# A two-layer-pair transformer kernel: the block before the last ends ahead of the last at six norms, and the last block goes by halves of the tokens

## The reference, cut to what matters

```python
def rms_norm(x, g):
    xf = x.astype(jnp.float32)
    y = xf * lax.rsqrt(jnp.mean(xf * xf, axis=-1, keepdims=True) + RMS_EPS) * g.astype(jnp.float32)
    return y.astype(x.dtype)
...
        h = h + mix_out
        h = h + conv_glu_ffn(rms_norm(h, norm_ffn_g[layer]), ffn_up[layer], ffn_conv_w[layer],
                             ffn_conv_b[layer], ffn_down[layer])
...
        h = h + g1 * y_lat
        h = h + g2 * conv_ffn(modulate(rms_norm_2(h, norm_ffn[i]), sh2, sc2), ffn_w_up[i], ffn_conv[i], ffn_w_down[i])
```

## Time and profile before

| | |
|---|---|
| median of 3 runs | 3118.66 us (3114.68 to 3126.62) |
| profiled execution, its own time | 3126.0 us |
| its span in the trace | 3124.2 us |
| mean granted TensorE clock | 0.978 of full speed |
| TensorE matmuls busy | 3029.7 us, 97% of the span |
| VectorE, ScalarE, GpSimd busy | 58%, 42%, 17% |
| memory traffic | 284.32 MB, mean 91 GB/s |

### The profile page before, as it was taken

The page is one execution under the profiler, slowest core; times in us unless marked ns, Lnnn a source line. Parts: engine busy times, 40 slices in busy tenths (PEclk is TensorE's granted clock), DMA queues, the critical chain, the costliest instruction groups (busy, mean ns, idle before and its releaser), DMA issues.

```text
span 3124.2 us, 46510 instructions
## 1 busy us (share of the span) xinstructions
PE 3029.7 (97%) x19324; PEld 2667.5 (85%) x19324; DVE 1822.9 (58%) x2664; ACT 1309.7 (42%) x2229; POOL 519.5 (17%) x464
## 2 busy tenths in 40 slices
PE   6999999999999999999999999998999999999999
PEld 6987878799999989998999987666888878878887
DVE  7675545448858563563876865664544543365353
ACT  4464555524323254673322355553332332343232
POOL 0002222123203200001311322101211201112020
PEclk9899989899999999999999999999999999999999
DMA  3210000014545422003554542101222222223222
GB/s 107 77 50 35 1 1 1 36 48 169 185 154 188 131 103 88 8 1 130 183 183 163 180 153 68 41 1 54 95 95 88 93 91 94 97 79 98 86 93 94
DMA packets 79554, 284.32 MB, mean 91 GB/s; under 512 B 8528, under 2 KB 9296, under 8 KB 78576
## 3 DMA queue, kind: packets, MB, share of 16 engines
q1 hardware_dynamic: 79344, 281.35, 27.1%
HBM read 274.96 MB, written 6.36 MB: 90 GB/s over the span
## 4 chain that ended last, share of the span: by engine, by line
PE 92%; DVE 4%; ACT 2%; issue 1%; DMA 0%; POOL 0%; SPq 0%; DVEq 0%; ACTq 0%; POOLq 0%
PE psum L345 64%; PE psum L2611 2%; PE psum L1193 2%; PE psum L839 2%; PE psum L1783 2%; PE psum L1214 2%; PE psum L1984 2%; PE psum L1225 1%; PE psum L1222 1%; PE psum L1966 1%; PE psum L1957 1%; PE psum L782 1%; DVE xt L682 1%; PE psum L2605 1%; PE psum L503 1%
## 5 line engine op out<-in xcount | busy, mean ns | idle before, releaser
L302 DVE TENSOR_TENSOR wlo<-wraw,whi 128x1024 fp32r<-128x1024 f32 (+2 forms) x398 | 508.6, 1299 | 629.7 <-ACT whi L295 620.6
L295 ACT CAST whi<-wraw 128x1024 fp32r<-128x1024 f32 (+2 forms) x398 | 396.2, 1022 | 515.4 <-PE psum L345 483.5
L426 DVE CUSTOM_DVE_ANT_0 araw<-araw,cond 128x1024 f32<-128x1024 f32 x112 | 181.2, 1655 | 0.0
L345 PE MATMUL psum<-f0xh,whi 128*128 128x264 f32 x704 | 143.8, 286 | 5.5 <-DVE f0xl L540 3.9
L345 PE MATMUL psum<-f1xh,whi 128*128 128x258 f32 x704 | 142.4, 284 | 5.6 <-DVE f1xl L540 3.8
L345 PE MATMUL psum<-f2xh,whi 128*128 128x512 f32 x352 | 140.1, 398 | 4.2 <-DVE f2xl L536 4.2
L345 PE MATMUL psum<-f3xh,whi 128*128 128x512 f32 x352 | 139.9, 397 | 4.2 <-DVE f3xl L536 4.2
L345 PE MATMUL psum<-f0xh,wlo 128*128 128x264 f32 x704 | 143.4, 285 | 0.0
L345 PE MATMUL psum<-f0xl,whi 128*128 128x264 f32 x704 | 143.0, 285 | 0.0
L345 PE MATMUL psum<-f1xh,wlo 128*128 128x258 f32 x704 | 142.3, 284 | 0.0
L345 PE MATMUL psum<-f1xl,whi 128*128 128x258 f32 x704 | 141.9, 283 | 0.0
(11 more groups left out here) (509 smaller groups left out, 8605.7 us busy)
## 6 DMA issues: line engine op xcount, KB each, us to landing
wraw<-d_w SPq DMA_DIRECT2D x357, 512.0 KB, 3.3
araw<-d_ada SPq DMA_DIRECT2D x112, 512.0 KB, 3.3
wraw<-d_w SPq DMA_DIRECT2D x32, 384.0 KB, 3.4
hn<-d_h SPq DMA_DIRECT2D x4, 528.0 KB, 7.6
hres<-d_h SPq DMA_DIRECT2D x1, 2112.0 KB, 8.5
spill<-hres SPq DMA_DIRECT2D x1, 2112.0 KB, 7.4
hres<-spill SPq DMA_DIRECT2D x1, 2112.0 KB, 9.1
cond<-d_cond SPq DMA_DIRECT2D x2, 1024.0 KB, 4.8
```

Source lines behind the costliest of these rows:

```text
L295: e.copy(whi[0:rows, n % NH, 0:kt * cols], wraw[0:rows, n % NR, 0:kt * cols]).then_inc(*w_hi.up(n))
L302: e.tensor_tensor(wlo[0:rows, n % NH, 0:kt * cols], wraw[0:rows, n % NR, 0:kt * cols], whi[0:rows, n % NH, 0:kt * cols].bitcast(F32), ALU. ...
L345: ins = e.matmul(psum[0:bw, b0 + nb * len(sl) + si, 0:ln], l_ if z == 2 else h_, (xp.lo if z == 1 else xp.hi)[:, k, o:o + ln], start=k == ...
L426: e.tensor_tensor_reduce(out=w, in0=w, in1=self.c[:, col, :], scale=1.0, scalar=0.0, op0=ALU.mult, op1=ALU.add, accum_out=ada[:, ly, blk, ...
```

## The change

Six parts, at the six norms that follow a projection (r0 is left as it is, but for its written form):

- In the last chunk of the last pair, TensorE goes through all k for block 6 first, then all k for block 7, and raises a semaphore of its own (`lin6`) when block 6 is complete.
- VectorE adds block 6 when `lin6` is up, and block 7 in two halves of the tokens, with a semaphore for the first half (`res7`).
- ScalarE squares block 7 in two halves.
- TensorE's sums go by halves of the tokens: the two halves of a sum have PSUM banks of their own at 512 tokens too, and the last sum waits for each half of the square alone and tells its first half (`n_ss7`).
- ScalarE's first logarithm waits for the first half of the sums, the second for the second.
- VectorE calls `ready` before it waits for the factor, and multiplies block 0 in two halves, each after its half of the factor.

```diff
@@ lin_pe
                     e.wait_ge(*w_lo.at(n))
-                    for i in range(cnt):
+                    apart = block6 is not None and j == pairs - 1 and k0 + cnt == kt
+                    for i, nb in sorted(((i, nb) for i in range(cnt) for nb in range(bpp)), key=lambda x: x[::-1] if apart else x):
                         k = k0 + i
-                        if j == 0:
+                        if j == 0 and nb == 0:
                             need(e, k)
...
+                        if apart and nb == 0 and i == cnt - 1:
+                            ins.then_inc(*lin6.up(block6))
                     ins.then_inc(*w_used.up(n))
@@ the squares and the root
+        LAST = {"f0": "wo", "sb": "f0b", "f1": "sbo", "f2": "wino", "sc": "f2b", "f3": "scout"}
...
+        def rms_square_last(e, t, src, sq, ntok):
+
+            e.wait_ge(*rms_added(t, 2))
+            half = ntok // 2
+            e.wait_ge(*res7.at(LAST[t]))
+            e.activation(sq[:, 2, 0:half], src(7)[:, 0:half], ACT.Square).then_inc(*n_sq7.up(t))
+            e.wait_ge(*res.at(LAST[t], 7))
+            e.activation(sq[:, 2, half:ntok], src(7)[:, half:ntok], ACT.Square).then_inc(*n_sq.up(t, 7))
+
         def rms_root(e, t, ntok, rt, bank):
-            e.wait_ge(*n_ss.at(t, 2))
             for h in range(2):
+                e.wait_ge(*(n_ss7.at(t) if t in LAST and not h else n_ss.at(t, 2)))
@@ the sums
         def rms_psum(ntok, bank, h):
+            return psum[:, bank + h, 0:ntok // 2]
+
+        def rms_pe(e, t, ntok, sq, bank):
             half = ntok // 2
-            return psum[:, bank + h, 0:half] if ntok > 512 else psum[:, bank, h * half:(h + 1) * half]
...
+                for h in range(2):
+                    if t in LAST and i == 2:
+                        e.wait_ge(*(n_sq.at(t, 7) if h else n_sq7.at(t)))
+                    elif not h:
+                        e.wait_ge(*(n_sq.at(t, 5 + i) if i else rms_added(t, 5)))
+                    ins = e.matmul(rms_psum(ntok, bank, h), ones, sq[:, i, h * half:(h + 1) * half], start=i == 0, stop=i == 2)
+                    if h:
+                        ins.then_inc(*n_ss.up(t, i))
+                    elif t in LAST and i == 2:
+                        ins.then_inc(*n_ss7.up(t))
@@ norm_dve
+            half = ntok // 2
+            ready(e)
+            e.wait_ge(*n_rf.at("rc", t, 0))
+            e.scalar_tensor_tensor(out=tmp[:, 0, 0:half], in0=src(0)[:, 0:half], scalar=gain(0), in1=rt[:, 0:half], op0=ALU.mult,
+                                   op1=ALU.mult).then_inc(*n_t0.up(t))
             e.wait_ge(*n_rf.at("rc", t, 1))
-            ready(e)
-            norm_t(e, t, src, rt, gain, tmp, 0)
+            e.scalar_tensor_tensor(out=tmp[:, 0, half:ntok], in0=src(0)[:, half:ntok], scalar=gain(0), in1=rt[:, half:ntok],
+                                   op0=ALU.mult, op1=ALU.mult).then_inc(*n_t.up(t, 0))
@@ add_dve and ffn_dve: the additions, now in one function
+        def add_block(e, t, tag, h_, ntok, gate, j, p, place):
+            nb = 2 * j + p
+            if nb == 6 and t in LAST.values():
+                e.wait_ge(*lin6.at(t))
+            else:
+                e.wait_ge(*w_used.at(last_chunk(tag, j)))
...
+            if nb == 7 and t in LAST.values():
+                half = ntok // 2
+                for i in range(2):
+                    hh = h_[:, 7, i * half:(i + 1) * half]
+                    pp = ps[:, i, :] if ntok > 512 else ps[:, 0, i * half:(i + 1) * half]
+                    up = res.up(t, 7) if i else res7.up(t)
```

More of the change, by code:

```diff
@@ L323, in __init__, with lin_pe @@
                 self.lo = put(name + "l", [rows, kt, ntok], F32R)
-        def lin_pe(e, tag, x, pairs, ntok, need, room, kt=8, bpp=2, set0=0, parts=None, sets=8, mid=None, after=None):
+        def lin_pe(e, tag, x, pairs, ntok, need, room, kt=8, bpp=2, set0=0, parts=None, sets=8, mid=None, after=None,
+                   block6=None):
             sl = parts or [(x, o, ln) for o, ln in splits(ntok)]
@@ L444, in program @@
         n_rf = sig("n_rf", [(s, t, h) for t in RMS for s in ("rt", "rc") for h in range(2)])
+        LAST = {"f0": "wo", "sb": "f0b", "f1": "sbo", "f2": "wino", "sc": "f2b", "f3": "scout"}
+        lin6 = sig("lin6", [(s,) for s in LAST.values()])
+        res7 = sig("res7", [(s,) for s in LAST.values()])
+        n_sq7 = sig("n_sq7", [(t,) for t in LAST])
+        n_ss7 = sig("n_ss7", [(t,) for t in LAST])
+        n_t0 = sig("n_t0", [(t,) for t in LAST])
         def rms_added(t, k):
@@ L483, in act, with rest @@
                     rms_square(e, self.t, self.src, self.sq, self.there, (0, 1) if j == 2 else range(2, 6))
-            def rest(self, e):
+            def rest(self, e, ntok):
                 e.preload_act_table_set("natural_log_exp_and_others")
-                rms_square(e, self.t, self.src, self.sq, self.there, (6, 7))
+                rms_square(e, self.t, self.src, self.sq, self.there, (6,))
+                rms_square_last(e, self.t, self.src, self.sq, ntok)
         def splits_and_squares(e, tag, sqs):
@@ L1587, in ffn_pe @@
                        lambda e, j: room(e, j, 15 * half + 11), kt=11, set0=15 * half + 11,
-                       mid=F.tail.pe if F.tail and half else None)
+                       mid=F.tail.pe if F.tail and half else None,
+                       block6=f + "b" if half and f + "b" in LAST.values() else None)
         def ffn_act(e, F, sqs, bias):
             f, ntok, lead = F.f, F.ntok, F.lead
-            sqs.rest(e)
+            sqs.rest(e, ntok)
             rms_root(e, f, ntok, F.rt, 0)
@@ L1840, in rounded @@
                     e.copy(xq.hi[:, k, :], nts[:, (8 * i + k) % 3, :]).then_inc(*b_hi.up(i, k))
-            sq_sb.rest(e)
+            sq_sb.rest(e, L)
             rms_root(e, "sb", L, rts, 0)
@@ L1890, in tiles_ @@
             def tiles_(i, ks):
-                normed(i, ks[0])
+                if i or ks[0]:
+                    normed(i, ks[0])
+                else:
+                    first()
                 for k in ks:
@@ L2080, in room @@
                     e.wait_ge(*res.at("sbo", 2 * (j - 2) + 1))
-            lin_pe(e, "sbo", XoT, 4, LT, lambda e, k: None, room, parts=[(XoT, T1 + o, ln) for o, ln in splits(LT)])
+            lin_pe(e, "sbo", XoT, 4, LT, lambda e, k: None, room, parts=[(XoT, T1 + o, ln) for o, ln in splits(LT)],
+                   block6="sbo")
         def sbo_act(e):
@@ L2773, in room2 @@
                 e.wait_ge(*sc_part(2 * (8 + j) + 1))
-            lin_pe(e, "scout", xo3, 4, LX, lambda e, k: e.wait_ge(*y_lo.at(k)), room2)
+            lin_pe(e, "scout", xo3, 4, LX, lambda e, k: e.wait_ge(*y_lo.at(k)), room2, block6="scout")
         def sc_act(e):
-            sq_sc.rest(e)
+            sq_sc.rest(e, LX)
             rms_root(e, "sc", LX, scrt, 0)
```

53 lines of the change are left out of this document (24 added, 29 removed).

## The result

| | before | changed |
|---|---|---|
| median of 15 runs each | 3122.36 us (3114.68 to 3134.01) | 3112.09 us (3104.96 to 3124.01) |
| profiled execution, its own time | 3126.0 us | 3109.89 us |
| span, granted clock | 3124.2 us, 0.978 | 3108.1 us, 0.982 |

The ratio is 0.9966, 95% interval 0.9954 to 0.9977: the changed kernel is 0.34% faster, 10.6 us (7.2 to 14.4). The ratio and its interval compare all runs of the two kernels; they are not the quotient of the two medians. The forecast was 3110, with a chain shorter by 8.5 us.

A forecast was written before the change was run, and what follows sets the result against it. TensorE, busy nearly all the span, carries 92% of the chain; norm waits leave it idle. Gains of 1.35 us at four norms and 1.55 at two make 8.5: 3118.66 - 8.5 gives 3110 us, range 3102 to 3117.

The forecast's parts named there:

- theory A: At the six norms: the gain is the chain's alone, each part worth its term; the clock falls behind every norm as before.
- block 6 apart: In the norm's sums: block 6's square leaves the path and TensorE's 0.65 us wait goes; 0.8 us a norm.
- block 7 by halves: Behind the projection: both half squares are hidden by the sums of blocks 0 to 6; gives nothing, costs nothing.
- sums and root by halves: Behind the sums: first logarithm is done when the second sum ends; 0.35 us a norm, between 0 and 0.47.
- block 0 by halves, gains early: Ahead of the next projection: block 0's first half overlaps the second exponential, 0.2 us; gains leave the path, 0.2 us twice.
- fifth: In TensorE's sums at f2: the instruction up to which 1.67 us passed from the first sum, for two instructions.
- The sums: TensorE's six sums at each norm would run in one piece of about 3.0 us, without waiting for block 6's square.
- The next work: Behind each norm the gain stays; a new TensorE wait in the next projection's first chunk would show the prediction wrong.
- 3.3 is nearest to the one that fell: Pauses behind the sums shrink to 3.3 or 3.4 us; clock fell after 3.37, held after 2.54; its cost taken as unchanged.
- the third rival: Behind the norms, half clock lasts longer, 10 us of work at each: 3126 us; chance 0.05.
- the one that the chain would not get shorter: At the norms, handoffs or a late block 6 leave 3.9 us or less: 3115 us or more; gain below 5 us 0.14.
- the clock would hold: Behind the norms, shorter pauses keep 2.4 GHz: 16 us, 3102.7 us if at all four that count; two or more 0.16.

The follow-up runs named there:

- experiment 1: Changed kernel with block 7, root and block 0 whole and gains waiting, so only block 6 goes apart: six norms 40.9 us, one run 3109.68 us.
- experiment 4: Changed kernel with block 7 added and squared whole, all else as changed: six norms 37.45 us, one run 3122.16 us.
- 3: Changed kernel with block 0 of the norm multiplied whole and the gains waiting for the factor again: six norms 38.3 us, one run 3120.45 us.
- experiment 10: The changed kernel once more, unedited, on one chip beside the kernel before: median 3113.22 us, ratio to before 0.9964, norms 37.0 us.
- experiment 2: Changed kernel without block 6 apart (last chunk in the old order), all else as changed: six norms 42.3 us, one run 3109.99 us.
- 7: Changed kernel, but VectorE adds block 6's square to the sum of squares and TensorE sums twice, not three times: 3107.93 us, ratio to before 0.9945.

## Why the prediction was right

The forecast was theory A, and A holds for the chain. That the median came within 2.1 us of the 3110 is in part luck: the median of before rose from 3118.66 us with 3 runs to 3122.36 with 15, and the gain in the time was 10.6 us instead of 8.5. What bears the forecast is the sum of its terms. Each term against what its experiment showed:

| step | forecast | measured |
|---|---|---|
| block 6 apart | 6 x 0.8 = 4.8 us | 4.9 us (experiment 1) |
| block 7 by halves | 0 | 0.4 us (4) |
| sums and root by halves | 6 x 0.35 = 2.1 us | 2.16 us (3 against 1) |
| block 0 by halves, gains early | 6 x 0.2 + 2 x 0.2 = 1.6 us | 1.28 us (3) |
| sum | 8.5 us | 8.72 us |

- **Block 6.** The mechanism and the size were right. Off the path it is by 1.2 us at f2, and removing it gives more than the idle time of 0.65, as the prediction had it. Neighbouring matmuls overlap by 0.16 us (at f2 each takes 0.59 and the next starts 0.43 later), and a wait breaks one overlap: 0.65 + 0.16 = 0.81. (For 512 tokens these are the second and third instructions; the prediction's "fifth" is that of 528.)
- **Block 7.** "This part gives nothing by itself" was off by 0.02 to 0.11 us a norm. The reason is the cover: the prediction had the sums of blocks 0 to 6 last 2.0 us, they last 1.73, and the whole square is there at 1.67, so close that the last sum loses 0.1 us at f2, sc and f3 (experiment 4). In halves it is there in time.
- **The root.** The first logarithm starts 0.4 us before the sums end, as said.
- **Block 0 and the gains.** The term for block 0 was a little too large: 0.18 us at three norms, 0.11 at sc. At f2 and f3, 0.31 less 0.11 to 0.18 leaves 0.13 to 0.20 for the gains, against the 0.2 of the text.
- **The sums.** They were written down as about 3.0 us in one piece; they take 2.75 to 2.83. This did not enter the gain, because the term was read from the difference of starts.
- **The next work.** No new wait appeared in the first chunk behind a norm. The stage from f0 to sb took 394.6 us instead of 396.0, with 3.4 us of half clock both times: 1.4 us, all that f0's norm gave.
- **The clock.** "3.3 is nearest to the one that fell" was right in this sense, that the clock fell behind all six norms. But the trace of before had a row of 2.71 us (ahead of the matmul on `xlh` at 1863.39), which the prediction doesn't name, and the clock fell behind it. "Unchanged" was right only roughly: 14.75 us of half clock at the four norms where it costs, in one profile of before, became 18.2 in one profile and 23.2 in the profile of experiment 10. At half speed that would be 1.7 to 4.2 us given back. The runs' own gain of 10.6 us (7.2 to 14.4) neither shows this loss nor excludes it.

The rows behind the third rival were read a little off: by the earlier trace rows the half clock ended at 181.2 and came back from 188.1 to 191.5. Its sum of 10 us is not touched by this.

Of the rivals, the one that the chain would not get shorter is refuted by the table. That the clock would hold did not come about; its mechanism is real, for a filled pause held the clock and was worth 0.21% (0.04 to 0.38) where 7.45 us, 0.24%, had been priced, but shortening by 0.6 us was not enough. The third, longer half clock, was there in part (6 us instead of 4.7 at f2, and in experiment 10 over 5.5 us at all four), far from the price at which the kernel would have become slower.

## What to carry to other kernels

Where a sum over blocks ends a stage, finish the blocks one after the other and let the last sum's own length cover the last block: only what is behind the final matmul is paid. Read such a gain from the intervals that the change touches, since here a stage that it does not touch moved by up to 18 us from profile to profile. Where an engine's clock falls behind a pause that cannot be removed, matmuls that nobody needs, placed in the pause, cost nothing on the path and here were worth 0.2 to 0.3%; that differs little from what the change gave, and their intervals overlap. Before a sum is taken away, ask what it covers, and count from a point ahead of every wait that could be new: two new waits took more than half of what two sums instead of three should have given.

## What the runs showed of the hardware

Behind pauses of 3.81 to 4.16 us the clock fell 12 of 12 times (the kernel before and experiment 1). Behind 3.27 to 3.80 us it fell 31 of 36 times (the changed kernel twice, and experiments 2, 3, 4 and 7); behind about 2 us, 2 of 6; behind filled pauses, with 0.5 to 1.0 us left, 0 of 24. One more pause, which nothing here changed, stands behind sums that have a wait of their own. In the kernel before it is

```profile
1863.39 0.47 PE L345 MATMUL psum<-xlh,whi 128*128 128x512 f32 x1 [2.71 <-DVE xll L536]
```

It lasts 2.70 to 2.72 us in all thirteen profiles; the clock fell behind it in 7 and held in 6. The same pause of 3.49 us had it hold at sc in experiment 2 and fall there in the changed kernel. So in this range the length alone doesn't decide; in these counts the share of falls rises with it. What else decides was not tried, and the forecast of "as before" was more certain in its words than it could be.

The Trainium skill ("TensorE: Matmul & The Clock Gate", "Why this matters for your kernels") advises against long idle gaps between bursts of matmuls. The trace agrees with the direction, by the 12 of 12 and the 0 of 24.

The half clock behind a norm came in two sizes: 2.9 to 3.4 us of work at some norms and 4.7 to 6.2 at others, in one and the same execution. Some of it began up to 1.5 us behind the first matmul (f1 in experiment 2).

The slower runs of one kernel are those with the lower mean granted clock (with 14 extra matmuls, 3111.2 us at 0.986 and 3131.2 at 0.978). What sets the amount of half clock in the scan, 26 to 58 us from profile to profile, was not tried.
